# The even block's last round: the parked tiles reloaded inside it, and its conv norm, gates and splits between the solve's steps

## The reference, cut to what matters

```
z = h @ even_w_in
a_val, a_glu, a_gate, r, k, v, wd, ad, b_gate = split_cols(z, EVEN_SIZES)
ya = conformer_conv(a_val, a_glu, conv_w, conv_vec) * silu(a_gate)
yb = rwkv7_mix(r, k, v, wd, ad, ...) * silu(b_gate)
x = x + gate * (concatenate([ya, yb], -1) @ even_w_out)
```

## Time and profile before

| | us |
|---|---|
| median of 3 runs | 3277.93 (3275.95 to 3285.04) |
| the profiled execution | 3284.26 |
| its span | 3282.4 |
| TensorE busy | 3088.3 (94%) |
| VectorE busy | 2182.3 (66%) |
| ScalarE busy | 1245.2 (38%) |
| GpSimd busy | 891.3 (27%) |
| mean granted clock of TensorE | 0.975 |
| round 9 starts / the barrier falls / the stage `eo` ends, on TensorE | 728.9 / 776.5 / 927.9 |

### The profile page before, as it was taken

The page is one execution under the profiler, slowest core; times in us unless marked ns, Lnnn a source line. Parts: engine busy times, 40 slices in busy tenths (PEclk is TensorE's granted clock), DMA queues, the critical chain, the costliest instruction groups (busy, mean ns, idle before and its releaser), DMA issues.

```text
span 3282.4 us, 39831 instructions
## 1 busy us (share of the span) xinstructions
PE 3088.3 (94%) x16114; PEld 2418.5 (74%) x16114; DVE 2182.3 (66%) x3483; ACT 1245.2 (38%) x1816; POOL 891.3 (27%) x550
## 2 busy tenths in 40 slices
PE   6789999997889899999999999999999999999997
PEld 3567777675667666777887788878888888888885
DVE  3689999872679966475789899746665444444454
ACT  3334444332334455333333366633223222233233
POOL 2344444320324310034355432232222111111100
PEclk9899999998989999999999999999999999999999
DMA  5221111324212111132233357676554333333331
GB/s 205 90 69 46 52 50 52 110 81 176 74 65 82 54 39 39 65 116 87 94 113 135 123 197 236 203 254 199 192 185 155 122 122 122 122 122 122 118 120 39
DMA packets 166471, 380.93 MB, mean 116 GB/s; under 512 B 10768, under 2 KB 77328, under 8 KB 166160
## 3 DMA queue, kind: packets, MB, share of 16 engines
q1 hardware_dynamic: 166288, 378.38, 34.5%
HBM read 319.09 MB, written 59.24 MB: 115 GB/s over the span
## 4 chain that ended last, share of the span: by engine, by line
PE 72%; DVE 20%; ACT 4%; DMA 2%; POOL 2%; issue 1%; SPq 0%; DVEq 0%; ACTq 0%; POOLq 0%
PE ps L707 20%; PE ps L709 19%; PE ps L708 19%; DVE rw L1756 4%; DVE oh L2317 2%; PE ps L1103 2%; PE ps L1031 2%; DVE at L2055 1%; DVE ai L2053 1%; PE ps L1011 1%; PE ps L883 1%; POOL wsp L2397 1%; DVE at L2043 1%; POOL pk L2509 1%; PE ps L1021 1%
## 5 line engine op out<-in xcount | busy, mean ns | idle before, releaser
L707 PE MATMUL ps<-hT,wsp 128*128 128x512 f32 x2016 | 828.9, 411 | 51.4 <-POOL wsp L2397 29.5
L2397 POOL TENSOR_TENSOR wsp<-ring,wsp 128x1024 fp32r<-128x1024 f32 x207 | 516.3, 2496 | 1094.8 <-ACT wsp L1160 1087.3
L709 PE MATMUL ps<-hT,wsp 128*128 128x512 f32 x2016 | 797.0, 395 | 0.0
L708 PE MATMUL ps<-hT,wsp 128*128 128x512 f32 x2016 | 795.6, 395 | 0.0
L707 PEld LDWEIGHTS ps<-hT,wsp 128*128 128x128 f32 x2016 | 384.5, 191 | 162.7 <-issue 23.4
L709 PEld LDWEIGHTS ps<-hT,wsp 128*128 128x128 f32 x2016 | 384.4, 191 | 84.1
L708 PEld LDWEIGHTS ps<-hT,wsp 128*128 128x128 f32 x2016 | 385.8, 191 | 78.3 <-issue 5.8
L2516 POOL TENSOR_TENSOR ex<-ex 128x512 fp32r<-128x512 f32 x128 | 176.0, 1390 | 833.6 <-ACT ex L1539 833.6
L1160 ACT ACTIVATE wsp<-ring 128x1024 fp32r<-128x1024 f32 x311 | 321.7, 1050 | 106.5 <-PE ps L709 79.7
L2341 DVE TENSOR_TENSOR xT<-ps,xT 128x512 f32<-128x512 f32 x256 | 175.0, 688 | 262.5 <-PE ps L709 262.5
L707 PE MATMUL ps<-ex 128*128 128x512 f32 x808 | 314.9, 390 | 2.0 <-DVE ex L1590 2.0
(11 more groups left out here) (393 smaller groups left out, 4773.2 us busy)
## 6 DMA issues: line engine op xcount, KB each, us to landing
ring<-in_eu SPq DMA_DIRECT2D x128, 512.0 KB, 3.3
ring<-in_ev SPq DMA_DIRECT2D x128, 512.0 KB, 3.6
gd<-oh SPq DMA_DIRECT2D x8, 4096.0 KB, 14.9
ex<-gd SPq DMA_DIRECT2D x32, 1024.0 KB, 6.6
ring<-in_ein SPq DMA_DIRECT2D x57, 512.0 KB, 3.3
ring<-in_oin SPq DMA_DIRECT2D x39, 512.0 KB, 3.2
ring<-in_ada SPq DMA_DIRECT2D x37, 512.0 KB, 3.3
ex<-zd SPq DMA_DIRECT2D x17, 1024.0 KB, 9.4
```

What stands on the lines that cost most here:

```text
L707: pe.matmul(out, W[0], R[0], start=first, stop=False)
L708: pe.matmul(out, W[0], R[1], start=False, stop=False)
L709: return pe.matmul(out, W[1], R[0], start=False, stop=last)
L2397: pool.tensor_tensor(s[:, 1, :], raw_of(i), s[:, 0, :].bitcast(F32), ALU.subtract).then_inc(pool_done, G.step("lo", i))
```

## The change

It has five parts.

- **Memory.** The tiles of `rw` are allocated in another order, so that those still needed in round 9 don't lie where `yb`, `yc`, `ag` and the scratch tiles of `eo` lie. `xr` is gone: the input is loaded into `xT` itself, once the solve has read its last matrices there.
- **`rw_left`.** A mark at the start of round 9. `left(w)` makes an engine wait until all four have come that far, and only then touch the tiles of `eo`.
- **Round 9.** SyncE loads `yc` at the mark, then `yb` (7 tiles) and `ag` (3 tiles, `STORED = 3`). The gate tiles 3 to 7 are all computed here and go straight to `ag`. Two new tables place the norm (`mean9`) and the splits of `yb` (`split9`). Tile 7 of `yb` is never parked.
- **The norm.** VectorE sums the eight tiles (`ysum`) and later the eight squares (in `ysub`), and TensorE makes one matmul for each sum. The mean is subtracted straight from the PSUM bank.
- **After it.** `eb` starts with no barrier ahead of it, with the rest of `lna` and `yas` between its first units. Its evictions (`ebx`) come two units later. The barrier `eo_begin` moves to the middle of `eb`, and the rope tables start there.

All tables in `PLACES` have other numbers, those of the other rounds for the same pieces as before.

```diff
-LATE = 6
+STORED = 3
 PLACES = {
-    "conv8": (29, 143, 143, 143, 293, 300, 300, 420, 424, 424, 516, 529, 529, 547, 547, 604, 604, 714, 736,
-        736, 747, 747, 800, 801, 807, 807, 834, 834, 894, 927, 927),
+    "conv8": (142, 154, 154, 298, 367, 371, 371, 371, 372, 380, 405, 405, 426, 426, 453, 538, 586, 586, 684,
+        690, 698, 698, 698, 698, 727, 745, 761, 761, 761, 812, 835),
...
+    "split9": (547, 566, 576, 587, 642, 656, 691),
...
         if i == 9:
-            lane = [*dense("bgate", 7, 56), *lane]
+            order.append(("rw_left",))
+            blocks = [*dense("bgate", 7, 56), *gates((3,)), *lane[:2], *gates((4,)), *lane[2:], *gates((5, 6, 7))]
+            lane = blocks
...
+        if i == 9:
+            at += placed([("load_yb",), ("load_ag",), *(("ysum", k) for k in range(1, 8)), ("lnm",),
+                          *(("ysub", k) for k in range(9)), ("lnv",), ("lns",), *(("lna", k) for k in range(3))], "mean9")
+            at += placed([("ybs", k) for k in range(7)], "split9")
...
-    order.append(("eo_begin",))
-    order += [("late", m, unit("ein", 16 + m)) for m in range(LATE, 8)]
-    order.append(("ybs",))
-    order.append(("eb", 0, unit("eout", 1)))
-    order.append(("lnm",))
-    order += [("eb", m, unit("eout", 2 * m + 1)) for m in (1, 2)]
-    order.append(("lnv",))
+    order += [("hT_free",), ("load_x",)]
     for m in range(8):
-        if m < 5:
-            order.append(("eb", 3 + m, unit("eout", 2 * m + 7)))
-        order.append(("lna", m))
+        order.append(("eb", m, unit("eout", 2 * m + 1)))
+        if m < 4:
+            order += [("lna", k) for k in ((3, 4), (5,), (6,), (7,))[m]]
+            order += [("yas", 2 * m), ("yas", 2 * m + 1)]
         if m >= 2:
-            order.append(("yas", m - 2))
-    order += [("yas", 6), ("yas", 7), ("tab_in",)]
+            order.append(("ebx", m - 2))
+        if m == 4:
+            order += [("eo_begin",), ("tab_in",)]
+        if m > 4:
+            order.append(("rope_tab", m - 5))
+    order += [("ebx", 6), ("ebx", 7)]
     for m in range(8):
         order.append(("ea", m, unit("eout", 2 * m)))
         order.append(("square", "n1", m))
-        if m < 7:
-            order.append(("rope_tab", m))
+        if m < 4:
+            order.append(("rope_tab", m + 3))
...
+        def left(w):
+            w.wait_ge(tensor_done, T("left"))
+            w.wait_ge(vector_done, V("left"))
+            w.wait_ge(scalar_done, A("left"))
+            w.wait_ge(pool_done, G("left"))
...
             def lnm():
-                out, free = all_b.open("lnm", A, "mu")
+                out, free = inv_b.open("lnm", V, "yc", 7)
                 w.wait_ge(*free)
-                w.wait_ge(yc_in, 16)
-                for m in range(8):
-                    r = pe.matmul(out, ones[:, :], yc[:, m, :], start=m == 0, stop=m == 7)
-                r.then_inc(tensor_done, T.step("lnm"))
+                w.wait_ge(vector_done, V("ysum", 7))
+                pe.matmul(out, ones[:, :], eot[3], start=True, stop=True).then_inc(tensor_done, T.step("lnm"))
...
+            def ysum(k):
+                left(w)
+                w.wait_ge(yc_in, 16)
+                own()
+                dve.tensor_tensor(eot[3], yc[:, 0, :] if k == 1 else eot[3], yc[:, k, :], ALU.add).then_inc(
+                    vector_done, V.step("ysum", k))
+
+            def ysub(k):
+                w.wait_ge(tensor_done, T("lnm"))
+                if k < 8:
+                    dve.scalar_tensor_tensor(out=yc[:, k, :], in0=inv_b.at["lnm"], scalar=-1.0 / D, in1=yc[:, k, :],
+                                             op0=ALU.mult, op1=ALU.add).then_inc(vector_done, V.step("yc", k))
+                if k >= 2:
+                    w.wait_ge(scalar_done, A("ysq", k - 1))
+                    own()
+                    dve.tensor_tensor(eot[3], eot[0] if k == 2 else eot[3], eot[(k - 1) % 3], ALU.add).then_inc(
+                        vector_done, V.step("ysq", k - 1))
...
+            def rw_left():
+                left(w)
                 for s in yt_out:
                     w.wait_ge(s, 64)
...
                 sp.dma_start(yc, t["yd"][0:8].rearrange("k p s -> p k s")).then_inc(yc_in, 16)
+            def load_yb():
+                w.wait_ge(gs_out, 16 * 7)
+                sp.dma_start(yb[:, 0:7, :], t["yd"][8:15].rearrange("k p s -> p k s")).then_inc(yb_in, 16)
...
+            def load_x():
+                w.wait_ge(tensor_done, T("y", 7, 3))
+                sp.dma_start(xT[:, :, :], t["xT"].rearrange("(k p) s -> p k s", p=128)).then_inc(x_in, 16)
```

More of the change, by code:

```diff
@@ L186, in solve @@
         return [*((s, c, q) for q in range(CH) for s in ("x1", "sa", "st")), ("gn1", c), ("gn2", c),
-                ("gn3", c), *(("gnr", c, i) for i in range(CH)), ("gn4", c)]
+                ("gn3", c), *(("gnr", c, i) for i in range(CH)), ("gn4", c), *([("ybs", 7)] if c == 7 else [])]
     def conv(m):
@@ L575, in build @@
         ga_out = [sem(f"s_ga{i}") for i in range(2)]
-        yb_in = [sem(f"s_yb{i}") for i in range(4)]
         pos_in, pcol_in, icnt_in, poolw_in, keys_in, io16_in = (
@@ L949, in lnm @@
             def lnm():
-                out, free = all_b.open("lnm", A, "mu")
+                out, free = inv_b.open("lnm", V, "yc", 7)
                 w.wait_ge(*free)
-                w.wait_ge(yc_in, 16)
-                for m in range(8):
-                    r = pe.matmul(out, ones[:, :], yc[:, m, :], start=m == 0, stop=m == 7)
-                r.then_inc(tensor_done, T.step("lnm"))
+                w.wait_ge(vector_done, V("ysum", 7))
+                pe.matmul(out, ones[:, :], eot[3], start=True, stop=True).then_inc(tensor_done, T.step("lnm"))
             def lnv():
-                out, free = all_b.open("lnv", V, "var")
+                out, free = inv_b.open("lnv", V, "var")
                 w.wait_ge(*free)
-                for m in range(8):
-                    w.wait_ge(scalar_done, A("ysq", m))
-                    pe.matmul(out, ones[:, :], eot[m % 3], start=m == 0, stop=m == 7).then_inc(
-                        tensor_done, T.step("lnv", m))
+                w.wait_ge(vector_done, V("ysq", 7))
+                pe.matmul(out, ones[:, :], eot[3], start=True, stop=True).then_inc(tensor_done, T.step("lnv"))
             def ea(m, n):
@@ L1139, in tensor_program @@
                   "freed": lambda tag: T.here("free", tag), "bcast": bcast, "ogs": lambda half: T.here("free", "ogs", half),
-                  "late": late, "ybs": lambda: T.here("free", "late"),
+                  "rw_left": lambda: T.here("left"), "hT_free": lambda: T.here("free", "gates"),
                   "yms": lambda: T.here("free", "ym"),
@@ L1368, in yas @@
             def yas(k):
-                w.wait_ge(tensor_done, T("free", "late"))
+                w.wait_ge(tensor_done, T("free", "gates"))
                 w.wait_ge(pool_done, G("ya", k))
@@ L1571, in scalar_program @@
                   "turn": turn, "tr": tr, "p1": p1, "odd": odd, "x1": x1, "sa": sa, "gn1": gn1, "gn3": gn3,
-                  "late": late, "ybs": ybs, "eb": eb, "lnm": lnm, "lnv": lnv, "lna": lna, "yas": yas, "ea": ea, "rope_tab": rope_tab,
-                  "ki": ahead_of, "wi": wi_, "qi": ahead_of, "key": key, "value": value, "values": values,
+                  "rw_left": lambda: A.here("left"), "ybs": ybs, "eb": eb, "ysub": ysub, "lns": lns, "lna": lna, "yas": yas, "ea": ea,
+                  "rope_tab": rope_tab, "ki": ahead_of, "wi": wi_, "qi": ahead_of, "key": key, "value": value, "values": values,
                   "index": index, "q": ahead_of, "turnq": turnq, "gate": gate, "logits": logits, "pt": pt, "ogs": ogs, "oo": ahead_of,
@@ L1582, in vector_program @@
             at = {"lo": 0, "hot": 0}
+            eb_at = {}
             def own():
@@ L2374, in vector_program @@
                   "p2": p2, "x1": x1, "st": st, "gnr": gnr, "gn4": gn4,
-                  "late": ahead_of, "ybs": ybs, "eb": eb, "lnm": lnm, "lnv": lnv, "lna": lna, "yas": yas, "ea": ea, "rope_tab": rope_tab,
+                  "rw_left": lambda: V.here("left"), "ybs": ybs, "eb": eb, "ebx": ebx, "ysum": ysum, "ysub": ysub, "lnv": lnv, "lns": lns, "lna": lna, "yas": yas, "ea": ea, "rope_tab": rope_tab,
                   "ki": ki, "qi": qi_, "key": ahead_of, "value": ahead_of, "index": index, "q": q_, "turnq": turnq,
@@ L2520, in pool_program @@
             walk({"ada": ahead_of, "dense": dense_part, "norm_nf": norm_nf, "mix": mix,
-                  "hats": hats, "xt0": xt0, "tr": tr, "p1": ab_odd, "lna": lna, "late": ahead_of, "eb": ahead_of, "ea": ahead_of, "ki": ki,
+                  "hats": hats, "xt0": xt0, "tr": tr, "p1": ab_odd, "rw_left": lambda: G.here("left"), "lna": lna, "eb": ahead_of, "ea": ahead_of, "ki": ki,
                   "qi": qi_, "key": key, "value": ahead_of, "q": ahead_of, "turnq": turnq, "gate": ahead_of, "look": look,
```

168 lines of the change are left out of this document (83 added, 85 removed), and 9 rows, old and new, of the table PLACES.

## The result

Timed side by side on one chip, the changed kernel took 3241.45 us (median of 4 runs, 3233.96 to 3245.33) and the kernel before 3280.68 us (4 runs): a ratio of 0.988 with an interval of 0.987 to 0.990. The forecast was 3239 us. The total came out right, but by luck: it has two errors of about 10 us each, in opposite directions, and they cancel.

The account below looks back on a forecast made before the run. TensorE was taken to be held by the stage-end barrier and VectorE's serial norm chain. 34.9 us from matmuls and waits, 4 from the tail and 0 from rounds 0 to 8 gave 39 off 3277.9: 3239 us, range 3222 to 3260.

Parts of the forecast that it names:

- x1 0 at 736.2 us in both kernels: Start of tile 7's solve on TensorE, behind the memset of `Sbd`: taken as 736.2 us before and after the change.
- rounds 0 to 8 … I count 0 (±6): Rounds 0 to 8, whose tables of places all changed: effect on the time counted as 0, within 6 us.
- rival C: Slower or even: new places cost in rounds 1 to 7, 5.6 us each eating the gain of 39; chance 0.05.
- common point: `x1` of tile 7, step 0, at 736.2 us: where the account of TensorE's work before and after starts.
- 138.7 us of matmuls: TensorE's work after the change, from tile 7's first `x1` to the last `ea`, without waits: 138.7 us.
- Waits of 10 us: TensorE's waits from tile 7's first `x1` to the last `ea`: terms summing to 9.7, taken as 10 us.
- `lnm`: TensorE's wait at the mean's matmul, after `yc` lands and seven sums: 0.9 us worked out, 1.5 counted.
- `lnv`: TensorE's wait at the variance's matmul: 1.3 us, plus 1.2 for GpSimd's splits, 2.5 us in all.
- the last tile of `yb`: TensorE's wait in the first `eb` for tile 7's group norm, copy and difference: 1.3 us worked out, 2.5 put.
- The tail: From the last `ea` to the next norm's first matmul: 8.1 us falls to 2.3 to 4.1, gain 4 us.
- Rival B: Round 9 becomes a chain of waits, 25 us instead of 10: gain 24, 3254 us; chance 0.14.
- E: More gain than forecast: waits are 3 us and the rounds before win 6 us, 3222 us; chance 0.07.

Follow-up runs that it names:

- e2: The changed kernel with all tables of rounds 0 to 8 at their old numbers: 3231.95 us, ratio 0.985 against the kernel before.
- e9: The changed kernel with the mean made by eight f32 matmuls on TensorE again, without VectorE's seven sums: 3246.31 us, ratio 0.9905 against the kernel before.
- e7: The changed kernel with the rope tables back at their old places, seven of them between the units of `ea`: 3244.9 us, ratio 0.9885 against the kernel before.
- e1: The changed kernel with the tables of rounds 0 to 7 back at their old numbers: 3225.56 us, ratio 0.983 against the kernel before.
- e6: The changed kernel with only the table `prep` back at its old numbers, one run: 3226.19 us.

## Why the prediction was right, and which terms were not

**x1 0 at 736.2 us in both kernels: wrong, by 9.2 us.** This is the step "rounds 0 to 8 … I count 0 (±6)". I looked at round 8, which indeed gained 3.1 us from memset to memset (TensorE's start of round 9 shows nothing of it), and took the moves in rounds 1 to 7 for a few places that cancel. They cost 14.6 us over six rounds, less 3.06 in round 8 and 3.25 of a first memset that came earlier, which is chance. That moves the clearing of `Sbd` by 8.3 us; the other 0.9 is that TensorE comes to `x1` only 1.2 us behind it, without waiting. It is rival C's mechanism at less than half its price, 2.4 us a round where 5.6 would have decided. The prediction's own test (the start of round 9 moving by more than 6 us) went off at 13.6. Its common point hid something else: with round 9 starting at 728.94 us and only 12 dense matmuls ahead, TensorE would have been there at 731.8 and waited 4.4 us for the memset, which stands in no list of waits. That wait shows as 2.22 us in e2 and not at all in the changed kernel, where the memset comes first.

**138.7 us of matmuls: about right.** TensorE was busy for 136.8 us up to the norm, gaps left out. Of the removed 12.3 us e9 confirms one half (5.8 for one of the two sums).

**Waits of 10 us: too many.** The last `ea` ended at 887.61 − 2.32 = 885.3, 139.9 us behind `x1` 0, where 148.7 was forecast. TensorE's waits from 736 to 900 us in the changed kernel:

```profile
PE ps L782 <- DVE msum L1649: 2.3, 1, 2.3
PE ps L981 <- DVE eo L1936: 1.5, 1, 1.5
...
PE ps L920 <- DVE small L1879: 0.8, 1, 0.8
PE ps L932 <- ACT small L1341: 0.4, 1, 0.4
PE ps L732 <- DVE eo L1904: 0.3, 1, 0.3
```

Without the first row, which is the tail, and the rows of the stages around, that is 3.0 us. Term by term: `lnm` 0 (forecast 1.5), `x1` 2 0.8 (1.0), `lnv` 1.5 (2.5), the split of a gate tile 0 (0.8), ScalarE's turnaround 0.4 (0.4), the last tile of `yb` 0.3 (2.5), leftovers 0 (1.0). The last tile of `yb` is the largest: by its rows the forecast had 1.3 us and put 2.5. At `lnm`, `yc` landed as forecast:

```profile
eo<-yd SPq DMA_DIRECT2D x1, 2048.0 KB, 8.9
```

but `x1` 1 came 11.9 us after `x1` 0 and `lnm` 2.8 us behind it, and VectorE was ready for both:

```profile
753.96 0.69 DVE L1924 TENSOR_TENSOR eo<-eo 128x512 f32<-128x512 f32 x1 [9.55 <-DMA eo<-yd]
755.28 4.32 DVE L1924 TENSOR_TENSOR eo<-eo 128x512 f32<-128x512 f32 x6
```

The six sums ended at 759.6, 0.5 us ahead of the matmul. And `lnv` had 1.2 us for collisions with splits, which the subtractions with their PSUM operand don't have.

**The tail: 5.8 us instead of 4.** The eviction, square and sum took their free durations, as no split met the sum; e7 shows that the tables' place is the cause.

**Together.** Forecast −34.9 − 4 + 0 = −38.9; measured at the norm −43.76 − 5.78 + 9.23 = −40.31. The median moved by 39.2 us. The forecast held by luck: 10.6 us too little gain and 9.2 us too little loss met, and the last `ea` stood near the forecast 885 us for the same reason. With the old tables, which the forecast took to be worth nothing, the kernel takes 3225.6 us (e1), 13 less than forecast. Rival B (a chain of waits in round 9) is refuted by the list of waits; E had the waits right (3 us) and the rounds before wrong; its two terms also add up to 3226 us, not 3222.

## What to carry to other kernels

A chain of small dependent instructions on one engine (sum, mean, difference, variance, normalize) is nearly free where the main engine has matmuls that need none of it, and is paid for where it stands next to its reader: here 38 us for the same instructions, 27 of them as waits and 11 as matmuls at the lower clock. When a change regenerates all numbers of a hand-placed order, time each part's table by itself: this one carried a loss of some 15 us in rounds that the change had no reason to touch, and setting them back gave the fastest version. And where an estimate sums many small waits, each counted "to be safe", the sum is biased upwards; give each the value that its rows give, and keep the safety for the range.

## What the runs showed of the hardware

Switching ScalarE's function cost 1.28 us of table load and nothing visible beside it: the activation before the load at 476.91 us ended at 476.89, and the one behind it started at 478.20. All 61 table loads of the changed kernel's trace took 1.28 us, and 46 of them were followed by the next activation within 0.02 us. The Trainium skill (ScalarE: Activation LUTs, section What ACT_TABLE_LOAD costs) gives about 2.66 us for a switch, the load and a drain; these rows show only the load.

GpSimd's split did not slow the VectorE instructions that read one operand from PSUM (1.29 us for two), but lengthened those with two SBUF operands (2.08 for two, and 2.71 for a tap that is 0.74 elsewhere in the same round). In e6 the same split, at 479.40 us, stood beside three reciprocals, which read one tensor: they took 0.89 to 0.94 us each, against 0.95 for the one ahead of the split.
